# Ten slab rests of the memory stage moved from VectorE to GpSimd (one core, fp32 in two halves)

## The chip, the cores and the metric

One core of one Trainium2 chip runs the whole kernel. The metric is the device time of one execution in microseconds (us). The kernel before was timed three times; the median is what the change is held against.

## The reference, cut to what matters

The model has two blocks of two layers each. In both layers of the second block the tokens attend to a memory of 256 rows, and the part of the reference that the change touches is the making of that memory's keys and values:

```python
def rmsnorm(x, g):
    y = x * lax.rsqrt(jnp.mean(x * x, axis=-1, keepdims=True) + EPS)
    return y * g

def mem_attention(xq, mem_n, w_mem_kv):      # mem_n (1, 256, 1024), w_mem_kv (1024, 1024)
    mk, mv = jnp.split(mem_n @ w_mem_kv, 2, axis=-1)   # keys and values, 512 columns each
    ...

def even_layer(h, mem_n, ...):               # odd_layer alike
    u = rmsnorm(h, g)                        # the next stage multiplies u
    ... xq, ... = split(u @ w_in)
    m = mem_attention(xq, mem_n, w_mem_kv)
```

`mem_n @ w_mem_kv` doesn't depend on `h`, so it is computed while the norm of `h` (512 tokens by 1024 features) is made ready.

## The kernel before, in words

**Products in halves.** Each fp32 product is three TensorE products of fp32r tiles: the high half of the weights by the high half of the input, high by rest, rest by high (`product`, L477 to L482). The high half is a rounded copy made by ScalarE; the rest is the value less the high half.

**The weight stream.** All weights pass through the core as one stream of 473 slabs of 128x1024 fp32. Four engines handle each slab n in turn. SyncE loads it into `ring` (three places, L406) once the rest of slab n-3 is made. ScalarE casts it into `w_hi` (three places, `high`, L432) once TensorE has finished slab n-3. An engine subtracts, `w_lo = ring - w_hi` ("the rest of the slab"), and signals `split_done`. TensorE waits for `split_done` (`slab`) and multiplies. So the casts and rests run up to three slabs ahead of TensorE. GpSimd makes the rests (`low` and `lows_upto`, L455), but ten of them are made by VectorE with `low_by_vector` (L465), and all ten are in the stage described next, five in each layer.

**The stage around the change** is `mem_keys_values` (L2315), once in each layer of the second block. It uses eight slabs: four of the keys (24 products of 256 columns each) and four of the values (12 products of 512 columns each). Call them slabs 0 to 7 of the stage, and slabs 8, 9 and 10 the first three of the next stage. When the stage begins, the rests of slabs 0 to 2 are made or under way, so the stage itself has to issue those of slabs 3 to 10. Before the change VectorE makes the rests of slabs 3 to 7 and GpSimd those of slabs 8, 9 and 10, after a wait for VectorE's last.

Nothing schedules the engines at run time: each runs its own list, in the order in which the program wrote it.

- VectorE: the last sums of squares of `h` (`Sums.add`, L611; add 1 to add 7, written by the stage before); rest of slab 3; the reciprocal of the norm's root (`invert`, L633); rest of slab 4; then for each of eight norm tiles c a **scale** (`scale`, L785: `h` by gain by `inv` into one of two `raw` buffers) and a **norm rest** (`rest`, L791: `raw` less its rounded copy, which makes `x_ready`), with the rests of slabs 5, 6 and 7 after norm rest 1, 3 and 5.
- ScalarE: the cast of a slab once TensorE is through with the slab three before it, the copy of a finished product out of PSUM (L2368, L2383), the square root of the sum (L627), and the **round** of each norm tile (L777), which waits for its scale. Rounds 0 and 1 stand ahead of the cast of slab 6, rounds 2 and 3 ahead of slab 7's, 4 and 5 ahead of slab 8's, 6 and 7 ahead of slab 9's.
- TensorE: slabs 0 and 1, then the sum over partitions (`total`, L619, which waits for add 7), then slabs 2 to 7.
- GpSimd: the rests of slabs 8, 9 and 10.

**The next stage** (`dense_f` with `paced`, called by `mem_attention`) multiplies slabs 8 and 9 by the normalised tiles, alternating the two slabs tile by tile. It can do three products with slab 8 and then needs slab 9. Tile c also waits for norm rest c.

```python
            for i in range(2):                                    # ScalarE, values
                k.high(act, first + nk + i + 1 + SPLIT)
                norm.round(act, 4 + 2 * i)
                norm.round(act, 5 + 2 * i)
```

Of the kernel before, what the change touches and what calls it, by code (L numbers as in the profile page):

```python
# [22 lines left out]
F32 = mybir.dt.float32  # L23
# [13 lines left out]
RING = 3  # L37
SPLIT = 3
# [244 lines left out]
class Signal:  # L283


    def __init__(self, handle):
        self.handle, self.base = handle, 0
# [26 lines left out]
class Core:  # L314


    def __init__(self, nc, ctx, dram):
        self.nc, self.dram = nc, dram
        self.ctx = ctx
        sb = lambda n, s, dt=F32: ctx.enter_context(nc.sbuf_tensor(n, s, dt))  # L320
        self.ring = sb("ring", [P, RING, SLAB])
        self.w_hi = sb("w_hi", [P, SPLIT, SLAB], F32R)
        self.w_lo = sb("w_lo", [P, SPLIT, SLAB], F32R)
        self.h = sb("h", [P, KT, SEQ])
        self.x_hi = sb("x_hi", [P, KT, SEQ], F32R)
        self.x_lo = sb("x_lo", [P, KT, SEQ], F32R)
        self.r_hi = sb("r_hi", [P, 2, SEQ], F32R)
        self.r_lo = sb("r_lo", [P, 2, SEQ], F32R)
        self.inv = sb("inv", [P, SEQ])
        self.mem_hi = sb("mem_hi", [P, KT, NMEM], F32R)  # L330
        self.mem_lo = sb("mem_lo", [P, KT, NMEM], F32R)
        self.cst = sb("cst", [P, CONST_N])
        self.vec = sb("vec", [P, VEC_TOTAL])
        self.arena_n = (nc.sbuf_top - nc.sbuf_base) // 4 - 8
        self.arena = sb("arena", [P, self.arena_n])
        self.ps = ctx.enter_context(nc.psum_tensor("ps", [P, 8, SEQ], F32))
        names = ("product_done", "evacuated", "squares_done", "pairs_done", "sum_done", "root_done", "vec_chain",
                 "pool_chain", "act_step", "dve_step", "pe_step", "pe_step2", "pool_step", "dve_read", "scores_done",
                 "biased", "exp_done", "diag_done", "turned", "turned_copied", "out_done", "out_copied", "tmp_ready",
                 "high_done", "split_done", "raw_done", "hi_done", "lo_done", "x_ready", "h_written", "row_part",  # L340
                 "row_done", "row_read", "conv_gated", "conv_done", "conv_copied", "conv_squared", "conv_silu", "mix_done", "inverted", "cmp_copied", "pool_copied", "row_high", "row_low", "cst_loaded", "vec_loaded", "bias_loaded", "feed_high", "feed_ready", "feed_squared", "feed_added",
                 "feed_summed", "feed_rooted", "feed_inverted", "gate_scaled", "up_scaled", "frev_negated", "frev_made", "frev_copied",
                 "lam_dots", "lam_sum", "lam_exp", "mem_squared", "mem_summed",
                 "mem_rooted", "mem_inverted", "mem_scaled", "mem_rounded", "mem_ready", "p_high", "p_low", "proj_done",
                 "proj_part", "proj_read", "rope_swapped", "rope_added", "roped")
        self.s = {n: Signal(ctx.enter_context(nc.semaphore(n))) for n in names}
        self.slab_loaded = [ctx.enter_context(nc.semaphore(f"slab_loaded{i}")) for i in range(RING)]
        self.x_loaded = [ctx.enter_context(nc.semaphore(f"x_loaded{i}")) for i in range(4)]
        self.aux = Signal(ctx.enter_context(nc.semaphore("aux_loaded")))
        self.stored = Signal(ctx.enter_context(nc.semaphore("stored")))  # L350
        self.cmp_loaded = [Signal(ctx.enter_context(nc.semaphore(f"cmp_loaded{i}"))) for i in range(2)]
        self.loaded = self.highs = self.lows = 0
        self.lows_taken = None
        self.slab_end = []
        self.early, self.early_after, self.late = [], [], []
        self.bank_read = [None] * 8
# [91 lines left out]
    def lows_upto(self, pool, upto):  # L448

        while self.lows < min(NSLAB, upto):  # L450
            n = self.lows
            if n == self.lows_taken:
                pool.wait_ge(self.s["split_done"].handle, n)
            pool.wait_ge(self.s["high_done"].handle, n + 1)
            self.nc.gpsimd.tensor_tensor(self.w_lo[:, n % SPLIT, :], self.ring[:, n % RING, :],  # L455
                                         self.w_hi[:, n % SPLIT, :].bitcast(F32),
                                         ALU.subtract).then_inc(self.s["split_done"].handle, 1)
            self.lows += 1

    def low_by_vector(self, dve):  # L460

        n = self.lows
        dve.wait_ge(self.s["split_done"].handle, n)
        dve.wait_ge(self.s["high_done"].handle, n + 1)
        self.nc.vector.tensor_tensor(self.w_lo[:, n % SPLIT, :], self.ring[:, n % RING, :],  # L465
                                     self.w_hi[:, n % SPLIT, :].bitcast(F32),
                                     ALU.subtract).then_inc(self.s["split_done"].handle, 1)
        self.lows = self.lows_taken = n + 1

    def slab(self, pe, n, *shape):  # L470

# [1843 lines left out]
def mem_keys_values(k, layer, ready, norm, sums):  # L2315

    nc, s = k.nc, k.s  # L2320
    mk, mv = k.at(MEM_KV[layer], 4, NMEM), k.at(MEM_KV[layer] + 1024, 2, 512)
    first, nk = STREAM_AT[f"mk{layer}"]
    groups = contraction_groups(512)
    assert STREAM_AT[f"mv{layer}"] == (first + nk, len(groups))
    n = nk + len(groups)
# [5 lines left out]
    with Stage(nc) as block:  # L2331
        @block.sync
        def _(sp):
            k.stream(sp)

        @block.tensor
        def _(pe):
            pe.wait_ge(*ready)
            for m in range(nk):
                hi, lo = k.slab(pe, first + m, P)  # L2340
                k.bank(pe, m)
                for c in range(KT):
                    ins = k.product(k.ps[:, m, 0:NMEM], (hi[:, c, :], lo[:, c, :]), (k.mem_hi[:, c, :], k.mem_lo[:, c, :]),
                                    c == 0, c == KT - 1)
                ins.then_inc(done.handle, 1)
                if m == 1:
                    sums.total(pe, 6)
            for i, (c0, cn) in enumerate(groups):
                hi, lo = k.slab(pe, first + nk + i, 512)
                for t in range(2):  # L2350
                    tok = slice(t * P, (t + 1) * P)
                    if i == 0:
                        k.bank(pe, nk + t)
                    for ci in range(cn):
                        c = c0 + ci
                        ins = k.product(k.ps[:, nk + t, :], (k.mem_hi[:, c, tok], k.mem_lo[:, c, tok]),
                                        (hi[:, ci, :], lo[:, ci, :]), c == 0, c == KT - 1)
                    if i == len(groups) - 1:
                        ins.then_inc(done.handle, 1)
                if i < len(groups) - 1:  # L2360
                    ins.then_inc(part.handle, 1)

        @block.scalar
        def _(act):
            for m in range(nk):
                act.wait_ge(done.handle, done.at(m + 1))
                k.high(act, first + m + 1 + SPLIT)
                nc.scalar.copy(mk[:, m, :], k.ps[:, m, 0:NMEM]).then_inc(read.handle, 1)  # L2368
                if m == 1:
                    sums.sqrt(act, 6)  # L2370
                if m >= 2:
                    norm.round(act, 2 * m - 4)
                    norm.round(act, 2 * m - 3)
            for i in range(2):
# [3 lines that stand above are left out]
            k.high(act, first + nk + 3 + SPLIT)  # L2378
            for t in range(2):
                act.wait_ge(done.handle, done.at(nk + t + 1))  # L2380
                if t == 1:
                    k.all_high(act)
                nc.scalar.copy(mv[:, t, :], k.ps[:, nk + t, :]).then_inc(read.handle, 1)  # L2383

        @block.vector
        def _(dve):
            assert k.lows == first + SPLIT
            k.low_by_vector(dve)
            sums.invert(dve)
            k.low_by_vector(dve)  # L2390
            norm.scale(dve, 0)
            for c in range(1, KT):
                norm.scale(dve, c)
                norm.rest(dve, c - 1)
                if c % 2 == 0:
                    k.low_by_vector(dve)
            norm.rest(dve, KT - 1)

        @block.gpsimd
        def _(pool):  # L2400
            k.low(pool)
# [506 lines left out]
```

## Time and profile before

| what | value |
|---|---|
| median of 3 runs | 3308.28 us (3301.98 to 3309.21) |
| the profiled execution's own time | 3297.97 us |
| its span, first to last instruction | 3296.6 us |
| busy: TensorE, VectorE, ScalarE, GpSimd | 96%, 41%, 35%, 35% |
| mean granted TensorE clock | 0.968 of full speed |

All times in rows are us from the span's start unless marked ns. The profiled execution is 10.3 us under the median. TensorE is busy for 96% of the span. The other engines matter where TensorE waits for them, and for the change that means two stretches: from about 2175 to 2210 (first layer of the second block) and from about 2608 to 2645 (second layer).

### The profile page before, as it was taken

To read this page: it belongs to the slowest core of one execution; us is meant where nothing else is said; L and a number is where in the kernel's file an instruction comes from. 1 tells how busy PE (TensorE), PEld (TensorE's weight loads), DVE (VectorE), ACT (ScalarE), POOL (GpSimd) and SP (SyncE) were. 2 spreads that over 40 slices of the span, in tenths; PEclk is the share of its full clock that TensorE was granted. 3 is DMA by queue.
4 is the path that set the end of the run, shared out by engine and by line. 5 is a ranking of instruction groups with operands and counts; after the bars stand their busy time and mean duration, and the time that the engine had idled before them with its cause. 6 is when DMAs were issued, how large, how long until landed. Compare 5 with 4: busy or idle time off the path is not lost.

```text
span 3296.6 us, 36185 instructions
## 1 busy us (share of the span) xinstructions
PE 3149.0 (96%) x14236; PEld 2514.4 (76%) x14236; DVE 1364.8 (41%) x2455; ACT 1168.3 (35%) x2028; POOL 1147.7 (35%) x480
## 2 busy tenths in 40 slices
PE   8999998989999999999989999989999989999998
PEld 6888776668888878887758888867758768876786
DVE  5311496844121451113964321367153423156442
ACT  4222464333222442223414232344323432345422
POOL 4444431014444444444414444433314332300143
PEclk9999998799999999999999999999999999979999
DMA  4333221003333323332303333333213334300032
GB/s 141 102 96 97 81 83 39 1 26 102 96 98 98 93 89 96 98 98 89 102 21 114 97 96 101 95 97 108 86 38 97 99 104 159 96 1 1 20 96 76
DMA packets 76524, 274.33 MB, mean 83 GB/s; under 512 B 8472, under 2 KB 9368, under 8 KB 75973
## 3 DMA queue, kind: packets, MB, share of 16 engines
q1 hardware_dynamic: 76356, 272.03, 26.6%
q8 instruction: 114, 1.87, 0.2%
q14 instruction: 54, 0.43, 0.0%
HBM read 269.85 MB, written 2.15 MB: 83 GB/s over the span
## 4 chain that ended last, share of the span: by engine, by line
PE 84%; DVE 11%; ACT 2%; issue 2%; POOL 1%; DMA 0%; SPq 0%; ACTq 0%; DVEq 0%; POOLq 0%
PE ps L480 23%; PE ps L481 23%; PE ps L482 23%; PE ps L1479 5%; PE ps L1453 4%; DVE arena L2101 3%; PE ps L1467 1%; PE ps L1465 1%; DVE arena L1735 1%; PE ps L2671 1%; PE ps L2533 1%; POOL w_lo L455 0%; ACT w_hi L432 0%; PE ps L2484 0%; DVE arena L1724 0%
## 5 line engine op out<-in xcount | busy, mean ns | idle before, releaser
L455 POOL TENSOR_TENSOR w_lo<-ring,w_hi 128x1024 fp32r<-128x1024 f32 x463 | 1131.9, 2447 | 2123.9 <-ACT w_hi L432 2082.4
L480 PE MATMUL ps<-x_hi,w_hi 128*128 128x512 f32 x2168 | 860.3, 397 | 34.2 <-POOL w_lo L455 21.1
L481 PE MATMUL ps<-x_lo,w_hi 128*128 128x512 f32 x2168 | 849.4, 392 | 0.0
L482 PE MATMUL ps<-x_hi,w_lo 128*128 128x512 f32 x2168 | 849.1, 392 | 0.0
L432 ACT CAST w_hi<-ring 128x1024 fp32r<-128x1024 f32 x473 | 493.9, 1046 | 746.7 <-PE ps L482 741.8
L480 PEld LDWEIGHTS ps<-x_hi,w_hi 128*128 128x128 f32 x2168 | 410.7, 189 | 128.4 <-issue 19.6
L481 PEld LDWEIGHTS ps<-x_lo,w_hi 128*128 128x128 f32 x2168 | 410.6, 189 | 88.6 <-issue 4.4
L482 PEld LDWEIGHTS ps<-x_hi,w_lo 128*128 128x128 f32 x2168 | 410.4, 189 | 86.6
L480 PE MATMUL ps<-r_hi,w_hi 128*128 128x512 f32 x1120 | 437.4, 391 | 11.5 <-issue 11.5
L481 PE MATMUL ps<-r_lo,w_hi 128*128 128x512 f32 x1120 | 436.7, 390 | 0.0
L482 PE MATMUL ps<-r_hi,w_lo 128*128 128x512 f32 x1120 | 436.5, 390 | 0.0
L1052 DVE TENSOR_TENSOR r_lo<-arena,r_hi 128x512 fp32r<-128x512 f32 x136 | 100.9, 746 | 566.8 <-ACT r_hi L1047 566.8
L1047 ACT CAST r_hi<-arena 128x512 fp32r<-128x512 f32 x136 | 83.8, 621 | 484.8 <-PE ps L482 484.8
L480 PEld LDWEIGHTS ps<-r_hi,w_hi 128*128 128x128 f32 x1120 | 211.0, 188 | 56.3 <-issue 12.3
L482 PEld LDWEIGHTS ps<-r_hi,w_lo 128*128 128x128 f32 x1120 | 210.9, 188 | 44.2
L481 PEld LDWEIGHTS ps<-r_lo,w_hi 128*128 128x128 f32 x1120 | 211.0, 188 | 43.5
L1309 DVE TENSOR_TENSOR arena<-ps,inv 128x512 f32<-128x512 f32 x88 | 60.9, 692 | 375.4 <-PE ps L482 375.4
L1281 ACT ACTIVATE arena<-arena 128x512 f32<-128x512 f32 x88 | 55.6, 632 | 408.5 <-DVE arena L1307 408.5
L1557 ACT ACTIVATE arena<-arena 128x256 f32<-128x256 f32 (+7 forms) x240 | 120.8, 504 | 215.4 <-DVE arena L1500 214.1
L1479 PE MATMUL ps<-arena 128*128 128x128 f32 (+3 forms) x1024 | 184.6, 309 | 12.7 <-ACT arena L1566 12.7
L1453 PE MATMUL ps<-arena 128*128 128x256 f32 (+11 forms) x480 | 173.8, 453 | 5.3 <-ACT arena L2417 3.4
L1307 DVE TENSOR_TENSOR arena<-ps,inv 128x512 f32<-128x512 f32 x88 | 60.8, 691 | 285.3 <-PE ps L482 285.2
(240 smaller groups left out, 3311.5 us busy)
## 6 DMA issues: line engine op xcount, KB each, us to landing
ring<-in_stream SPq DMA_DIRECT2D x473, 512.0 KB, 3.5
arena<-in_cmp_w SPq DMA_DIRECT2D x16, 512.0 KB, 4.5
arena<-frev SPq DMA_DIRECT2D x1, 3072.0 KB, 14.8
h<-in_x SPq DMA_DIRECT2D x4, 512.0 KB, 7.1
out<-arena SPq DMA_DIRECT2D x4, 512.0 KB
arena<-in_p SPq DMA_DIRECT2D x2, 512.0 KB
arena<-in_mem SPq DMA_DIRECT2D x1, 1024.0 KB
arena<-in_pool_recip SPq DMA_DIRECT2D x1, 1024.0 KB
```

Of the source, the lines that this page charges most:

```text
L432: self.nc.scalar.copy(self.w_hi[:, n % SPLIT, :], self.ring[:, n % RING, :]).then_inc(self.s["high_done"].handle, 1)
L455: self.nc.gpsimd.tensor_tensor(self.w_lo[:, n % SPLIT, :], self.ring[:, n % RING, :], self.w_hi[:, n % SPLIT, :].bitcast(F32), ALU.subtrac ...
L480: nc.tensor.matmul(out, a[0], b[0], start=start, stop=False)
L481: nc.tensor.matmul(out, a[0], b[1], start=False, stop=False)
L482: return nc.tensor.matmul(out, a[1], b[0], start=False, stop=stop)
L1047: k.nc.scalar.copy(k.r_hi[0:w, i % 2, :], self.x[0:w, self.order[i], :]).then_inc(self.his.handle, 1)
L1052: k.nc.vector.tensor_tensor(k.r_lo[0:w, i % 2, :], self.x[0:w, self.order[i], :], k.r_hi[0:w, i % 2, :].bitcast(F32), ALU.subtract).then_i ...
L1309: nc.vector.tensor_tensor(up[:, f % 2, :], k.ps[:, 2 * (f % 3) + 1, :], inv, ALU.mult).then_inc(up_scaled.handle, 1)
L1453: nc.tensor.matmul(k.ps[:, i % 4, 0:u.w], u.q, u.key, start=True, stop=True).then_inc(scored.handle, 1)
L1479: ins = nc.tensor.matmul(k.ps[0:v.shape[-1], 6 + g % 2, 0:P], v, pt[0:rows, i % 2, j * P:(j + 1) * P], start=(u.first and j == 0), stop=(u ...
L1557: nc.scalar.activation(ex[:, i % 5, 0:u.w], ex[:, i % 5, 0:u.w], ACT.Exp, bias=low[:, i % 5:i % 5 + 1], scale=-1.0, accum_out=tot[:, i % 5 ...
L2101: k.vlink(nc.vector.scalar_tensor_tensor(dst, src, tap_weight(c, tap), dst, ALU.mult, ALU.add))
```

## The change

The three calls of `low_by_vector` in the stage (one before the reciprocal, one after it, one in the loop) go, and so do the function and its bookkeeping. GpSimd's `low`, which always continues from the last rest issued, then makes the rests of slabs 3 to 10 in one sequence, as it does in every other stage. VectorE's list in the stage is the reciprocal, eight scales and eight norm rests. The arithmetic is the same.

```diff
             n = self.lows
-            if n == self.lows_taken:
-                pool.wait_ge(self.s["split_done"].handle, n)
             pool.wait_ge(self.s["high_done"].handle, n + 1)
             self.nc.gpsimd.tensor_tensor(self.w_lo[:, n % SPLIT, :], self.ring[:, n % RING, :],
                                          self.w_hi[:, n % SPLIT, :].bitcast(F32),
                                          ALU.subtract).then_inc(self.s["split_done"].handle, 1)
             self.lows += 1
-
-    def low_by_vector(self, dve):
-
-        n = self.lows
-        dve.wait_ge(self.s["split_done"].handle, n)
-        dve.wait_ge(self.s["high_done"].handle, n + 1)
-        self.nc.vector.tensor_tensor(self.w_lo[:, n % SPLIT, :], self.ring[:, n % RING, :],
-                                     self.w_hi[:, n % SPLIT, :].bitcast(F32),
-                                     ALU.subtract).then_inc(self.s["split_done"].handle, 1)
-        self.lows = self.lows_taken = n + 1
...
         @block.vector
         def _(dve):
-            assert k.lows == first + SPLIT
-            k.low_by_vector(dve)
             sums.invert(dve)
-            k.low_by_vector(dve)
             norm.scale(dve, 0)
             for c in range(1, KT):
                 norm.scale(dve, c)
                 norm.rest(dve, c - 1)
-                if c % 2 == 0:
-                    k.low_by_vector(dve)
             norm.rest(dve, KT - 1)
```

## Rows read from the trace of the kernel before

**Rows 1.** The page, part 4: shares of the chain that ended last.

```profile
PE 84%; DVE 11%; ACT 2%; issue 2%; POOL 1%; DMA 0%; SPq 0%; ACTq 0%; DVEq 0%; POOLq 0%
```

**Rows 2.** Tile w_lo on VectorE, and line 455 on GpSimd: durations in ns, min/median/max.

```profile
L465 DVE TENSOR_TENSOR w_lo<-ring,w_hi x10: 1224/1225/1227, 2179.7 to 2633.9; 128x1024 fp32r<-128x1024 f32 x10
...
L455 POOL TENSOR_TENSOR w_lo<-ring,w_hi x463: 2339/2398/2924, 9.3 to 3265.0; 128x1024 fp32r<-128x1024 f32 x155
```

**Rows 3.** Timeline of TensorE, instructions that waited: start, duration, [idle before <- releaser].

```profile
2186.80 0.50 PE L480 MATMUL ps<-w_hi,mem_hi 128*128 128x512 f32 x1 [0.23 <-DVE w_lo L465]
2191.49 0.50 PE L480 MATMUL ps<-w_hi,mem_hi 128*128 128x512 f32 x1 [1.68 <-DVE w_lo L465]
...
2205.10 0.47 PE L480 MATMUL ps<-x_hi,w_hi 128*128 128x512 f32 x1 [1.87 <-POOL w_lo L455]
...
2640.92 0.47 PE L480 MATMUL ps<-x_hi,w_hi 128*128 128x512 f32 x1 [1.88 <-POOL w_lo L455]
```

**Rows 4.** Timeline of VectorE, first layer: one turn of its list, and the reciprocal.

```profile
2182.13 3.35 DVE L633 RECIPROCAL inv<-arena 128x512 f32<-128x512 f32 x1 [1.25 <-ACT arena L627]
...
2190.21 1.22 DVE L465 TENSOR_TENSOR w_lo<-ring,w_hi 128x1024 fp32r<-128x1024 f32 x1
2191.35 0.74 DVE L785 SCALAR_TENSOR_TENSOR arena<-h,vec,inv 128x512 f32<-128x512 f32 x1
...
2194.12 1.23 DVE L465 TENSOR_TENSOR w_lo<-ring,w_hi 128x1024 fp32r<-128x1024 f32 x1
```

**Rows 5.** Timeline of ScalarE, first layer: casts of slabs 5, 6, 9 and a table load.

```profile
2180.11 1.28 ACT L627 ACT_TABLE_LOAD   x1
...
2183.81 1.05 ACT L432 CAST w_hi<-ring 128x1024 fp32r<-128x1024 f32 x1 [1.71 <-PE ps L482]
...
2188.63 1.05 ACT L432 CAST w_hi<-ring 128x1024 fp32r<-128x1024 f32 x1
...
2200.49 1.05 ACT L432 CAST w_hi<-ring 128x1024 fp32r<-128x1024 f32 x1
```

**Rows 6.** Timelines of GpSimd and VectorE where the two meet, first layer.

```profile
2175.67 2.67 POOL L455 TENSOR_TENSOR w_lo<-ring,w_hi 128x1024 fp32r<-128x1024 f32 x1 [2.96 <-ACT w_hi L432]
2199.34 8.40 POOL L455 TENSOR_TENSOR w_lo<-ring,w_hi 128x1024 fp32r<-128x1024 f32 x3 [21.00 <-DVE w_lo L465]
...
2176.15 3.47 DVE L611 TENSOR_TENSOR arena<-arena 128x512 f32<-128x512 f32 x2
...
2199.18 0.75 DVE L785 SCALAR_TENSOR_TENSOR arena<-h,vec,inv 128x512 f32<-128x512 f32 x1
2199.84 5.66 DVE L791 TENSOR_TENSOR x_lo<-arena,x_hi 128x512 fp32r<-128x512 f32 x2
```

**Rows 7.** Timelines elsewhere: a reciprocal and a GpSimd rest at the same time.

```profile
381.11 3.35 DVE L744 RECIPROCAL inv<-arena 128x512 f32<-128x512 f32 x1 [4.72 <-ACT arena L720]
...
382.08 2.34 POOL L455 TENSOR_TENSOR w_lo<-ring,w_hi 128x1024 fp32r<-128x1024 f32 x1 [2.91 <-ACT w_hi L432]
```

**Rows 8.** Lines 785 and 667, both scalar_tensor_tensor: ns, min/median/max.

```profile
L785 DVE SCALAR_TENSOR_TENSOR arena<-h,vec,inv x32: 745/753/755, 384.5 to 2635.0; 128x512 f32<-128x512 f32 x32
...
L667 DVE SCALAR_TENSOR_TENSOR x_lo<-h,vec,x_hi x8: 740/744/2866, 7.7 to 16.9; 128x512 fp32r<-128x512 f32 x8
```

**Rows 9.** Timelines, second layer: the seven adds and the rest of slab 2.

```profile
2608.18 7.10 DVE L611 TENSOR_TENSOR arena<-arena 128x512 f32<-128x512 f32 x7
...
2612.16 2.56 POOL L455 TENSOR_TENSOR w_lo<-ring,w_hi 128x1024 fp32r<-128x1024 f32 x1 [6.44 <-ACT w_hi L432]
```

**Rows 10.** The page, part 6: the stream's loads: KB each, median us to landing.

```profile
ring<-in_stream SPq DMA_DIRECT2D x473, 512.0 KB, 3.5
```

**Rows 11.** Stretches: window, its us, TensorE busy (instructions), granted clock, DMA share, GB/s.

```profile
2202.90:2205.10 2.20, 0.33 (x3) 1.00 0.80 229
2206.30:2209.50 3.20, 3.20 (x9) 0.51 0.64 189
...
2641.00:2645.00 4.00, 4.00 (x18) 1.00 0.64 149
```

More of the change, by code:

```diff
@@ L352, in __init__ @@
         self.loaded = self.highs = self.lows = 0
-        self.lows_taken = None
         self.slab_end = []
```

## The prediction

> **What bounds the kernel now.** I began with the chain that ended last: TensorE holds 84% of it and VectorE 11% [rows 1]. So outside the change's two stretches nothing can move, and inside them only what makes TensorE wait counts. The timeline of TensorE comes next. TensorE needs 4.69 - 1.68 = 3.0 us for a slab of the values and then stands still until VectorE's rest arrives; and at the start of the next stage it waits 1.87 and 1.88 us for GpSimd's rest of slab 9, at 2205.10 and 2640.92 [rows 3]. These two starts are the yardstick of the whole forecast: everything after them hangs on them, everything before is inside them.
>
> What sets their time is a loop of two engines. VectorE's turn (slab rest, scale, norm rest, scale, norm rest) takes 2194.12 - 2190.21 = 3.91 us [rows 4], and ScalarE's next cast stands behind the two rounds that this turn feeds. Casts 6 to 9 come once in 3.91 to 4.0 us ((2200.49 - 2188.63) / 3 = 3.95) [rows 5]. A slab rest fills 1.14 us of the turn, from its start to the next scale [rows 4].
>
> **A property of the two engines that decides the case** is in the rows where they meet. A GpSimd rest takes 2.40 us alone (median) [rows 2]. At 2175.67 one started while VectorE was in an add; it took 2.67. The two adds behind it took 3.47 and end at 2179.62, 1.28 after GpSimd's end (2178.34): both ran after it, at some 0.6 to 0.7 each [rows 6]. At 2199.34 three GpSimd rests took 8.40, 2.80 each, and two norm rests took 5.66, 2.83 each [rows 6]. So the two run one at a time and take turns: VectorE's tile waits out the GpSimd rest (ends 0.55 after it), GpSimd's next rest, already waiting, waits out that tile (0.4), and goes ahead of VectorE's next. A reciprocal reads a single tile of SBUF, and ran 3.35 us beside a GpSimd rest of 2.34, neither longer than alone [rows 7].
>
> **The change, part by part.** Removed: ten VectorE rests of 1.225 us = 12.3 us [rows 2], with their waits. Added: ten GpSimd rests of 2.40 = 24 us. GpSimd has the time (it stood idle 21.00 us before 2199.34 [rows 6]); the question is whom it holds up. Removing alone would cut VectorE's turn to 3.91 - 1.14 = 2.77 us. But a turn now has a GpSimd rest in it. I replay the lists of the engines with the durations above and the rule of turns. The same replay of the kernel before gives 2205.08 and 2640.95 for the two starts, measured 2205.10 and 2640.92 [rows 3].
>
> First layer:
> - Rest 3 is issued on GpSimd at 2178.4, right behind rest 2. Add 6 is ahead of it, so it runs 2178.8 to 2181.2, and add 7 waits it out: it ends at 2181.7 instead of 2179.6. The sum on TensorE and slab 2 start 2.1 later. ScalarE's root waited for its table until 2180.11 + 1.28 = 2181.39 before [rows 5], and now comes right after the sum, 2183.0, so the reciprocal ends 1.6 later, at 2187.05 (was 2182.13 + 3.35 = 2185.48 [rows 4]).
> - Slab 2's later end puts cast 5 at 2185.9 (was 2183.81 [rows 5]). Rest 5 runs 2187.0 to 2189.4, just before scale 0 wants to start at 2187.1; scale 0 ends at 2190.0. Scale 1, rounds 0 and 1 and cast 6 follow: cast 6 ends at 2192.3 (was 2188.63 + 1.05 = 2189.68 [rows 5]). +2.6.
> - Now the turn: cast ends; GpSimd waits for the norm rest in progress (0.35); rest 2.40; the blocked scale 0.62; its round 0.62, less 0.1 of overlap; cast 1.05. Sum 4.9 to 5.0 instead of 3.95. Three turns bring cast 9's end to 2207.0 (was 2200.49 + 1.05 = 2201.54). +5.5.
> - Rest 9 starts at once, 2207.1 to 2209.5 (before it queued behind rest 8 and a norm rest, which gives 1.0 back). TensorE starts at 2209.6. **+4.5.**
>
> Second layer:
> - Here rest 2 itself (2612.16, 2.56) already holds add 7: seven adds take 7.10 [rows 9]. Rest 3 comes after add 7. No loss on the sum; rests 3 and 4 run beside sum and reciprocal, which are not held up [rows 7].
> - Rest 5 (2622.6 to 2625.0) holds norm rest 0, and rest 6, waiting, goes ahead of scale 2 (2625.4 to 2627.8). Cast 7 ends at 2631.4, 1.9 later. Two turns of 4.9 bring cast 9 to 2641.2, then rest 9 to 2643.6 and TensorE to 2643.8. **+2.9.**
>
> TensorE's products are hidden in this: a slab of the values takes 3.0 us of a 4.9 us turn. The norm tiles are ready in time: the last norm rest would end near 2206.8 and 2640.9, before the starts. SyncE's loads wait for the rest three slabs back, which moves: slab 6's goes out at 2181.2 and is needed at 2191, slab 9's goes out at 2195 and is needed at 2206; a load lands 3.5 us after its issue [rows 10], so this queue costs nothing. No DMA is added and no queue is passed; the later engines only shift.
>
> **TensorE's clock.** After 2.2 us almost without work the clock was 0.51 of full speed (the 1.2 GHz level of 2.4) from 2206.30 to 2209.50, nine products where 3.2 / 0.227 = 14 fit at the full rate of one in 0.227 us: some 1.6 us lost. In the second layer TensorE stood 1.88 us and the clock stayed at 1.00 [rows 3, 11]. After the change it would stand about 4 us before each start. The first layer has the loss already; the second gets it new. Bounds 0 (the second layer's row) and +1.6 (the first's); I take +1.5, by the first row, as 4 us is nearer to 2.2 than to 1.9. Half clock inside the stage is covered by the turn's slack of 1.9 us.
>
> **Sum:** 4.5 + 2.9 + 1.5 = +8.9 us. Against the profiled execution that is 3297.97 + 8.9 = 3306.9; that execution lies 10.3 under the median, which is outside even the lowest run, so I put the difference on the median: 3308.28 + 8.9 = 3317.2, +0.27%. About 0.2% (6.6 us) is what a measurement of this kernel can tell from no change.
>
> **What before doesn't show** is a scale (L785) held up by GpSimd: 32 of them took 745 to 755 ns [rows 8]. Bounds: not held up, and not holding GpSimd, gives +1.9 and +0.9 in the replay, 2.8 in all; held up gives 7.4. I take the latter: L667 is the same instruction, also with two tiles in SBUF, and has one of 2866 ns; and the GpSimd rest that met a scale at 2199.34 was in a group of three at 2.80 each [rows 6, 8]. The Trainium skill ("SBUF — State Buffer", section "Who interferes with whom") says that a VectorE instruction with two SBUF inputs excludes a GpSimd instruction that reads SBUF, whatever its operation; by that the scale is held up, and no row of a blocked L785 is there to agree.
>
> **Rivals.**
> - *Scales slip past* (chance 0.17): +2.8, with 0 to 1.5 of clock, 3311 to 3313. For: L785's even durations. Against: L667.
> - *No clock loss in the second layer* (0.13): 7.4, 3315.7.
> - *An unlucky meeting in the second layer* (0.12): if add 6 ends just after rest 2 is issued rather than as now, or cast 3 comes while an add waits, rest 3 gets in front of add 7 as in the first layer. The point is where the adds stand against rest 2, some 0.4 us of shift. The replay then gives +5.0 instead of +2.9: 11.0 in all, 3319.3.
> - *Faster: the turns of VectorE and GpSimd interleave without blocking* (0.08). VectorE has 2.77 us of work in a turn, GpSimd 2.40; if the tiles fall into GpSimd's gaps, or the blocking seen is rarer than the rule says, the turn falls to TensorE's own 2.9 to 3.0 and the stage is 4.7 us shorter in each layer: -9.4, 3298.9. It decides if less than about a quarter of the tiles in the loop are blocked: a turn gains 1.14 and loses some 2.2 with each blocked scale. For: GpSimd waits for a cast each time, so it has gaps. Against: the cast comes exactly when VectorE has the next scale ready, so they meet in every turn; and the meetings in [rows 6] all cost the full wait.
> - *The change doesn't do what it says* (0.02): GpSimd's rests would stay 463.
>
> **How the numbers follow.** The forecast itself has 0.48. Slower: 0.44 of it (the rest is lost to the runs' own spread), the unlucky meeting's 0.12 and half of the case at 7.4, 0.07: 0.63. Faster: 0.08. Same: 0.29, the slipping scales above all. Range: from 2.8 less half the spread of the runs, 3.6, to 11.0 plus as much: 3307 to 3323, which leaves out the faster rival and tails.
>
> **What would show each step.** GpSimd's L455 x473, L465 gone. In the first layer an add of 2.7 us or more near 2179 and the reciprocal 1.6 later. L785 with a maximum near 2.9 us and about eight blocked ones; casts 6 to 9 about 4.9 apart; the next stage's first wait 4 us long, on GpSimd, at 2209.6 and (with the first layer's shift) 2648.3; clock 0.5 after both. I am wrong if casts stay 3.9 apart or less, or if L785 stays at 755 ns.

## The result and the profile after

The changed kernel takes 3309.13 us (median of 13 runs, 3303.43 to 3312.32), the kernel before in the same series 3301.98 (13 runs, 3299.35 to 3309.21). The ratio is 1.0020, with a 95% interval of 1.0012 to 1.0029: slower, by 4 to 9.6 us. The forecast was +8.9 us and 3317.2; the medians are 7.15 us apart. In a later series it was 1.0021 (1.0012 to 1.0031). The profiled execution took 3310.14 us with a span of 3308.8, against 3297.97 and 3296.6 before.

The line numbers have moved by up to 20: 455 is 452 now, 785 is 772, 791 is 778, 633 is 620, 611 is 598, 432 is 431, 480 is 467. The first fence has the answer to [rows 2] and [rows 8], by line and in ns (min/median/max): GpSimd's rests, the scales and the norm rests.

```profile
L452 POOL TENSOR_TENSOR w_lo<-ring,w_hi x473: 2337/2397/3144, 9.8 to 3277.2; 128x1024 fp32r<-128x1024 f32 x158
...
L772 DVE SCALAR_TENSOR_TENSOR arena<-h,vec,inv x32: 746/754/2895, 385.7 to 2646.1; 128x512 f32<-128x512 f32 x32
...
L778 DVE TENSOR_TENSOR x_lo<-arena,x_hi x32: 677/683/2474, 387.1 to 2649.5; 128x512 fp32r<-128x512 f32 x32
```

GpSimd makes all 473 rests, 2.40 us each as before. No scale was above 755 ns before; now the longest is 2895. The timeline of VectorE in the first layer answers to [rows 4] and [rows 6]:

```profile
2181.43 5.50 DVE L598 TENSOR_TENSOR arena<-arena 128x512 f32<-128x512 f32 x2
2189.37 3.35 DVE L620 RECIPROCAL inv<-arena 128x512 f32<-128x512 f32 x1 [2.45 <-ACT arena L614]
2192.76 1.42 DVE L772 SCALAR_TENSOR_TENSOR arena<-h,vec,inv 128x512 f32<-128x512 f32 x2
2194.52 2.47 DVE L778 TENSOR_TENSOR x_lo<-arena,x_hi 128x512 fp32r<-128x512 f32 x1 [0.34 <-ACT x_hi L764]
2197.03 2.77 DVE L772 SCALAR_TENSOR_TENSOR arena<-h,vec,inv 128x512 f32<-128x512 f32 x1
...
2203.21 2.72 DVE L772 SCALAR_TENSOR_TENSOR arena<-h,vec,inv 128x512 f32<-128x512 f32 x1
2205.86 0.68 DVE L778 TENSOR_TENSOR x_lo<-arena,x_hi 128x512 fp32r<-128x512 f32 x1
2206.57 0.75 DVE L772 SCALAR_TENSOR_TENSOR arena<-h,vec,inv 128x512 f32<-128x512 f32 x1
2207.24 0.68 DVE L778 TENSOR_TENSOR x_lo<-arena,x_hi 128x512 fp32r<-128x512 f32 x1
2207.96 2.73 DVE L772 SCALAR_TENSOR_TENSOR arena<-h,vec,inv 128x512 f32<-128x512 f32 x1
```

The same stretch on GpSimd (its rests of slabs 2 to 10 begin at 2180.95):

```profile
2180.95 8.19 POOL L452 TENSOR_TENSOR w_lo<-ring,w_hi 128x1024 fp32r<-128x1024 f32 x3 [2.96 <-ACT w_hi L431]
2193.77 2.67 POOL L452 TENSOR_TENSOR w_lo<-ring,w_hi 128x1024 fp32r<-128x1024 f32 x1 [4.64 <-ACT w_hi L431]
2196.65 2.60 POOL L452 TENSOR_TENSOR w_lo<-ring,w_hi 128x1024 fp32r<-128x1024 f32 x1 [0.21 <-ACT w_hi L431]
2202.87 2.52 POOL L452 TENSOR_TENSOR w_lo<-ring,w_hi 128x1024 fp32r<-128x1024 f32 x1 [3.62 <-ACT w_hi L431]
2207.62 2.52 POOL L452 TENSOR_TENSOR w_lo<-ring,w_hi 128x1024 fp32r<-128x1024 f32 x1 [2.23 <-ACT w_hi L431]
```

Read the two side by side: each of the rests of slabs 5 to 8, the last four of these lines, holds up exactly one tile of VectorE. The rest at 2207.62 starts while a norm rest is in progress (until 2207.92), takes 2.52 us, 0.12 more than one alone, and ends at 2210.14; the scale of 2207.96 ends 0.55 after it, at 2210.69. Two scales and two norm rests, which took 2.77 us without a slab rest, now fill 2207.96 - 2203.21 = 4.75 us. The casts of slabs 5 to 9 on ScalarE are the answer to [rows 5]; from cast 7 on they follow that beat:

```profile
2192.64 1.05 ACT L431 CAST w_hi<-ring 128x1024 fp32r<-128x1024 f32 x1 [3.37 <-PE ps L469]
...
2195.52 1.05 ACT L431 CAST w_hi<-ring 128x1024 fp32r<-128x1024 f32 x1 [0.52 <-PE ps L469]
...
2201.75 1.04 ACT L431 CAST w_hi<-ring 128x1024 fp32r<-128x1024 f32 x1
...
2206.49 1.04 ACT L431 CAST w_hi<-ring 128x1024 fp32r<-128x1024 f32 x1
...
2211.25 1.04 ACT L431 CAST w_hi<-ring 128x1024 fp32r<-128x1024 f32 x1
```

TensorE's starts with slab 9, in both layers, answer to [rows 3]:

```profile
2214.85 0.77 PE L467 MATMUL ps<-x_hi,w_hi 128*128 128x512 f32 x1 [3.68 <-POOL w_lo L452]
...
2652.96 0.77 PE L467 MATMUL ps<-x_hi,w_hi 128*128 128x512 f32 x1 [3.68 <-POOL w_lo L452]
```

In the second layer it is scale 1 (in the group of two at 2630.93) and scale 2 that the first two rests of the loop hold up:

```profile
2631.40 2.54 POOL L452 TENSOR_TENSOR w_lo<-ring,w_hi 128x1024 fp32r<-128x1024 f32 x1 [2.29 <-ACT w_hi L431]
2636.18 2.56 POOL L452 TENSOR_TENSOR w_lo<-ring,w_hi 128x1024 fp32r<-128x1024 f32 x1 [2.23 <-ACT w_hi L431]
...
2630.93 3.56 DVE L772 SCALAR_TENSOR_TENSOR arena<-h,vec,inv 128x512 f32<-128x512 f32 x2
...
2636.52 2.77 DVE L772 SCALAR_TENSOR_TENSOR arena<-h,vec,inv 128x512 f32<-128x512 f32 x1
```

The stretches behind the starts answer to [rows 11]; between TensorE's column and the clock stand weight loads, VectorE, ScalarE and GpSimd:

```profile
2214.85:2218.00 3.15, 3.15 (x8) 2.47 (x9) 0.00 (x0) 0.00 (x0) 2.18 (x1) 0.50 0.45 166
...
2652.96:2656.00 3.04, 3.04 (x7) 2.45 (x8) 0.00 (x0) 0.00 (x0) 2.18 (x1) 0.50 0.58 175
2656.00:2659.00 3.00, 3.00 (x9) 2.30 (x8) 0.00 (x0) 0.00 (x0) 0.00 (x0) 0.56 0.63 178
```

The wait is 3.68 us instead of 1.87, and after it the clock is 0.50 in both layers, and still 0.56 from 2656 to 2659.

**Where the 12.2 us between the two spans are.** A table load of ScalarE in the stage ahead of the first stretch comes at 2143.71 where it came at 2138.45, 5.26 us later, although the lists of the engines are the same up to there. The largest step is between the table loads at 520.11 and 683.88 before, 521.68 and 691.21 after (1.57 us later at its start, 7.33 at its end; some is given back later). Here are the two stretches, of before and then of after (us, TensorE busy, granted clock, DMA share, GB/s):

```profile
520.11:683.88 163.77, 150.87 (x765) 0.82 0.00 1
```

```profile
521.68:691.21 169.53, 157.10 (x765) 0.79 0.00 1
```

The same 765 instructions take 5.8 us longer at a lower granted clock. The changed lines don't set this: the stretch takes 163.8 us in e9, 166.4 to 166.5 in e1, e4 and e6, and 169.4 to 169.6 in all the other runs, and kernels built on the one before (e9, e1, e2) stand at all three levels. Whether it changes from one execution of a program to the next or goes with the program is not shown: the changed kernel was profiled twice and had 169.5 both times. So I don't compare spans but distances that the change can alter: **from the start of GpSimd's rest of slab 2 to TensorE's start with slab 9**, and from there to the table load of the attention (the clock's part). For before these are 2205.10 - 2175.67 = 29.43 and 2640.92 - 2612.16 = 28.76; after, 2214.85 - 2180.95 = 33.90 and 2652.96 - 2621.46 = 31.50. The change costs 4.47 and 2.74 us there. From start to table load it was 24.66 and 23.04 us and is 24.61 and 25.65.

The distance isn't free of the clock either. In the second layer of the kernel before the clock fell ahead of the sum; in e1 and e9, which have the same lists there, it didn't, and their distances are 28.04 and 27.98 instead of 28.76. The same stretch after rest 2 in the kernel before and then in e1:

```profile
2615.00:2619.00 4.00, 3.62 (x12) 0.58 0.71 184
```

```profile
2621.00:2625.00 4.00, 3.49 (x24) 1.00 0.67 161
```

So a difference of less than a microsecond between two distances can be the clock's. The changed kernel's profiles have such a fall in the second layer too, so its 2.74 compares like with like.

All kernels in one table; 23.0 in the clock columns is the value without a fall of the clock.

| kernel | distance, first layer | second layer | start to table load, first | second | median, us | ratio to before |
|---|---|---|---|---|---|---|
| before | 29.43 | 28.76 | 24.66 | 23.04 | 3300.7 to 3302.1 | 1 |
| the change | 33.90 | 31.50 | 24.61 | 25.65 | 3309.13 | 1.0020 (1.0012 to 1.0029) |
| the change again | 33.95 | 31.49 | 24.59 | 25.67 | 3308.33 | 1.0021 (1.0012 to 1.0031) |
| e1: first layer only | 34.01 | 28.04 | 24.55 | 23.02 | 3306.11 | 1.0016 (1.0006 to 1.0025) |
| e2: second layer only | 29.34 | 31.28 | 24.66 | 24.44 | 3306.64 | 1.0016 (1.0007 to 1.0025) |
| e3: norm's tiles in PSUM | 26.43 | 22.54 | 23.00 | 23.04 | 3288.40 | 0.9961 (0.9948 to 0.9973) |
| e5: inverse root in PSUM | 32.00 | 29.15 | 25.49 | 25.40 | 3305.81 | 1.0012 (1.0003 to 1.0021) |
| e8: adds first | 31.46 | 31.11 | 25.76 | 24.57 | 3309.57 | 1.0023 (1.0013 to 1.0033) |
| e7: filler | 33.91 | 30.90 | 23.07 | 23.05 | 3305.92 | 1.0012 (1.0004 to 1.0021) |
| e4: only slab 4 | 28.19 | 27.84 | 23.03 | 23.02 | 3295.29 | 0.9979 (0.9970 to 0.9987) |
| e6: PSUM, adds first | 23.79 | 23.54 | 23.00 | 23.01 | 3286.26 | 0.9952 (0.9938 to 0.9966) |
| e9: before with filler | 29.31 | 27.98 | 23.06 | 23.05 | 3298.36 | 0.9992 (0.9983 to 1.0001) |

### The profile page after: what moved, and what is told of

It reads as the page before. It is cut to its first block, busy times and chain, and to the rows that moved or that the text cites. A ratio compares the mean times of both kernels' runs of the same rounds, so it can differ in the third digit from the quotient of the medians.

```text
span 3308.8 us, 36175 instructions
## 1 busy us (share of the span) xinstructions
PE 3153.6 (95%) x14236; PEld 2519.3 (76%) x14236; DVE 1366.0 (41%) x2445; ACT 1167.8 (35%) x2028; POOL 1171.3 (35%) x490
## 3 DMA queue, kind: packets, MB, share of 16 engines
q8 instruction: 114, 1.87, 0.2%
## 4 chain that ended last, share of the span: by engine, by line
PE 84%; DVE 11%; ACT 2%; issue 1%; POOL 0%; DMA 0%; SPq 0%; ACTq 0%; DVEq 0%; POOLq 0%
PE ps L467 23%; PE ps L469 23%; PE ps L468 23%; PE ps L1466 5%; PE ps L1440 4%; DVE arena L2088 3%; PE ps L1454 2%; PE ps L1452 1%; DVE arena L1722 1%; PE ps L2651 1%; DVE arena L772 1%; PE ps L2513 1%; ACT w_hi L431 1%; PE ps L2464 0%; DVE arena L1711 0%
## 5 line engine op out<-in xcount | busy, mean ns | idle before, releaser
L452 POOL TENSOR_TENSOR w_lo<-ring,w_hi 128x1024 fp32r<-128x1024 f32 x473 | 1155.5, 2445 | 2112.4 <-ACT w_hi L431 2112.4
```

## The experiments

**Each layer alone (e1, e2).** VectorE keeps its rests in one layer: `low_by_vector` takes the slab's number and does nothing for slabs that aren't in a set, which holds slabs 3 to 7 of one layer.

```diff
-            k.low_by_vector(dve)
+            k.low_by_vector(dve, first + 3)      # returns if the slab isn't in by_vector
             sums.invert(dve)
```

e1, expected:

> The change in the first layer alone. Yardstick of every run: the distance from the start of GpSimd's rest of slab 2 to TensorE's start with slab 9, 29.43 us in the first and 28.76 us in the second layer before, 33.90 and 31.50 after. My theory (GpSimd and VectorE take turns at the tiles that read SBUF twice): first layer 33.9, second 28.8, time +4 to +5 us. Rival (the loss is TensorE's clock, lost wherever TensorE idles longer): first layer's distance as after, but hardly any time, since the clock fell there before too.

e2, expected:

> The change in the second layer alone. My theory: distances 29.4 and 31.5; time +2.7 us and whatever the clock takes, 0 to 2.6. If the clock were the larger part, this run would cost more than the first layer alone; if the turns are, less.

Measured: the distance grows only in the layer that is changed, by 4.6 and 2.5 us, as the whole change has it. In e1 the unchanged second layer has 28.04 where 28.8 was expected, by the clock as said above. The times (+0.16% each, 4.1 and 4.6 us) don't tell the layers apart: their intervals are 6 us wide. The rival of e1 (only the clock costs) has against it that e1's ratio is above 1 while its clock columns are those of before.

**The norm's tiles in PSUM (e3).** Keys of slabs 2 and 3 go to the upper halves of banks 0 and 1, so banks 2, 3 and 7 are free for the two raw tiles and the inverse root.

```diff
+    norm.raw, norm.inv = k.ps[:, 2:4, :], k.ps[:, 7, :]
...
-                    ins = k.product(k.ps[:, m, 0:NMEM], ...
+                    ins = k.product(k.ps[:, m % 2, m // 2 * NMEM:(m // 2 + 1) * NMEM], ...
...
-            sums.invert(dve)
+            sums.invert(dve, k.ps[:, 7, :])
```

> The changed kernel, but the inverse root and the two raw tiles of the norm lie in PSUM, so that a scale and a norm rest read SBUF once each. Same instructions on GpSimd, each of 2.40 us. Turns theory: nothing of the norm waits for GpSimd any more (L772 and L778 back at 0.7 to 0.8 us), only the adds do: distances 25.5 and 23.5 us, time 8 to 11 us under before, 15 or more under the change. Rival (the loss is GpSimd's longer rest on the path cast, rest, product: 2.40 for 1.23): the rests stay as long and on the same path, so the distances stay at 33 to 34 and 31 to 32 and the time at +7.

This is the run that decides between the two theories. GpSimd's work is that of the changed kernel. Timelines of VectorE and GpSimd, first layer:

```profile
2196.34 0.69 DVE L778 TENSOR_TENSOR x_lo<-ps,x_hi 128x512 fp32r<-128x512 f32 x1
2197.07 0.76 DVE L772 SCALAR_TENSOR_TENSOR ps<-h,vec,ps 128x512 f32<-128x512 f32 x1
2197.74 0.68 DVE L778 TENSOR_TENSOR x_lo<-ps,x_hi 128x512 fp32r<-128x512 f32 x1
2198.46 0.76 DVE L772 SCALAR_TENSOR_TENSOR ps<-h,vec,ps 128x512 f32<-128x512 f32 x1
2199.12 0.68 DVE L778 TENSOR_TENSOR x_lo<-ps,x_hi 128x512 fp32r<-128x512 f32 x1
...
2195.63 2.42 POOL L452 TENSOR_TENSOR w_lo<-ring,w_hi 128x1024 fp32r<-128x1024 f32 x1 [0.47 <-ACT w_hi L431]
2198.36 2.42 POOL L452 TENSOR_TENSOR w_lo<-ring,w_hi 128x1024 fp32r<-128x1024 f32 x1 [0.31 <-ACT w_hi L431]
2201.08 2.41 POOL L452 TENSOR_TENSOR w_lo<-ring,w_hi 128x1024 fp32r<-128x1024 f32 x1 [0.30 <-ACT w_hi L431]
```

Tiles and rests overlap freely, at 0.7 and 2.4 us, and the rests come every 2.73 us, which is TensorE's own 12 products of 0.227. The distances shrink by 7.5 and 9.0 us against the changed kernel. The rival would have left them. They are 26.43 and 22.54 where 25.5 and 23.5 were expected: in the first layer the clock fell twice ahead of the loop, in the second not at all, which may be the reason. The kernel is 0.39% faster than the one before, 13.7 us where 8 to 11 were expected; its stretches account for 10.9 of them (3.0 and 6.2 of distance, 1.7 of clock), and the rest isn't traced. No run puts the norm's tiles in PSUM in the kernel before, so how much of the gain needs the moved rests is not shown. Against the change it comes to 3288.40 - 3309.13 = -20.7 us: 7.5 + 9.0 of distance, 1.6 + 2.6 of clock.

**Only the inverse root in PSUM (e5).** Of the diff above only what concerns `inv`.

> The changed kernel with only the inverse root in PSUM: a scale reads SBUF once, a norm rest still twice. Turns theory: L772 never over 0.8 us, L778 takes the waits now; distances 30.9 and 29.2, time +1 to +4 us over before. Rival (GpSimd's longer rest): 33.9 and 31.5, +7.

By line and form (busy us, mean ns): the scales of the stage take 748 ns as in any other stage, and the norm rests of all stages 1052 on average where 683 is a free one; they take the waits. In the timelines eight norm rests of the two layers take 2.09 to 2.21 us.

```profile
L778 DVE TENSOR_TENSOR x_lo<-arena,x_hi 128x512 fp32r<-128x512 f32 x32 | 33.7, 1052 | 1.1 <-ACT x_hi L764 0.9
...
L772 DVE SCALAR_TENSOR_TENSOR arena<-h,vec,ps 128x512 f32<-128x512 f32 x16 | 11.8, 748 | 0.5
```

The distances are 32.0 and 29.15 (expected 30.9 and 29.2), 1.9 and 2.35 less than the change's. The first is a miss by 1.1 us. Its place can be told: rest 5 starts 12.84 us after rest 2, as with the change (12.82), and from there to TensorE's start it is 19.16 us in both layers, where the change had 21.08 and 21.56. So the loop gives back less in the first layer than I expected, and rest 2 to rest 5 is as it was.

The Trainium skill says (page "SBUF — State Buffer", section "Who interferes with whom") that a VectorE instruction with at most one SBUF input, outside its two-port modes, doesn't contend with GpSimd, and one with two contends with a GpSimd instruction that reads SBUF. The runs agree for this pair of operations: 2895 ns at most for a scale with two, at most 756 ns for each of e3's 16 with one.

**Adds first (e8).**

```diff
         def _(pool):
+            pool.wait_ge(sums.added.handle, sums.added.at(KT - 1))
             k.low(pool)
```

> The changed kernel with one wait more: GpSimd starts the stage's rests only when VectorE's last add is done. Tests the first step of my working, that rest 3 gets in front of add 7 in the first layer and costs 2.1 us there. Theory: first layer's distance 33.9 - 2.1 = 31.8, second unchanged at 31.5 (there rest 3 comes after add 7 anyway), time +5 over before. Rival (add 7's delay is covered elsewhere): 33.9.

The first distance is 31.46, 2.4 less than with the change; the second 31.11. The reciprocal begins 6.39 us after rest 2 instead of 8.42, so the meeting of rest 3 and add 7 costs about the 2.1 us that were said, in the first layer alone. TensorE waits 1.20 us for the sum instead of 3.24, and its clock doesn't fall on slab 2 (1.00 from 2185.2 to 2189.2), so the clock has a part in the 2.4. The time doesn't show it: 3309.57, 7.4 over before where 5 were expected; the interval of the ratio is 6 us wide, and the clock columns sum to the same as for the change.

**Filler (e7, e9).** Spare products into an unused bank while TensorE waits: 12 in the changed kernel, 6 in the one before. They are no part of the result.

```diff
+                        if (c, m) == (0, 1):
+                            k.bank(pe, 7)
+                            for i in range(4):               # 2 in e9
+                                k.product(k.ps[:, 7, :], (hi[:, 0, :], lo[:, 0, :]), (k.x_hi[:, 0, :], k.x_lo[:, 0, :]), True, True)
                         hi, lo = k.slab(pe, first + m, P)
```

> The changed kernel, but TensorE fills the wait for slab 9's rest with 12 spare products (2.7 us) into an unused bank. The extra products are no part of the result. Tests the clock term: with the products the granted clock after the start is 1.00 in both layers instead of 0.50; distances as in the changed kernel (33.9, 31.5), the time after the starts 1.7 us (first) and 2 to 2.6 us (second) shorter, time +2 to +4 over before. Rival (the clock's fall there isn't set off by the wait, or the rows after the start aren't bound by TensorE): time as in the changed kernel, +7.

The two stretches after the starts in e7 (us, TensorE busy, granted clock, DMA share, GB/s), against 0.50 in the changed kernel:

```profile
2214.32:2218.00 3.68, 3.68 (x16) 1.00 0.62 155
2650.95:2654.00 3.05, 3.04 (x13) 1.00 0.61 177
```

From start to table load both layers have 23.1 us now, so the fall of the clock cost 1.5 and 2.6 us in the changed kernel, and the wait sets it off. The median is 3.2 us under the change's (2.4 under that of the change again), 3.8 over before, as expected. The second distance is 30.90 where 31.5 was expected: here the first rest of the loop meets norm rest 0 and not scale 1, as in e2 (31.28) and e8 (31.11).

> The kernel before, with 6 spare products (1.4 us) in TensorE's wait of 1.87 us for slab 9. They are no part of the result. Open is why the changed kernel costs 7 us on average while its stretches in one profile are 9.8 us longer. Theory A: the kernel before loses 1.6 us of clock after the second start too in most executions, and its profile showed a lucky one; then the filler takes 3 us or more off the median. Theory B: it loses only after the first, as in its profile; then 1.6 us. Distances as before in both, 29.4 and 28.8; from the start to the attention's table load 23.0 us in both layers.

e9 has 23.06 and 23.05 us, its clock 1.00 after both starts, and its ratio is 0.9992 (0.9983 to 1.0001): -2.3 us, between theory A's 3 and theory B's 1.6. It doesn't decide. The profiles speak for B as far as they go: behind a second layer with the lists of before, the start to table load is 23.04 (before) and 23.02 (e1), no fall in either. Two profiles can't say how often it falls.

**Only slab 4 (e4).** The set of VectorE's slabs is 3, 5, 6, 7 in both layers.

> The kernel before with one of five rests moved in each layer: GpSimd makes that of slab 4, while VectorE is in the reciprocal; VectorE keeps 3, 5, 6 and 7. Theory (a rest costs only where it meets a tile that reads SBUF twice, and a reciprocal doesn't): the 1.14 us of rest 4 leave VectorE's list for nothing: distances 28.3 and 27.7, time -2 us. Rival (every rest moved to GpSimd costs its 1.2 us more): distances 30.6 and 30.0.

Timelines of GpSimd and VectorE, first layer:

```profile
2183.51 2.40 POOL L458 TENSOR_TENSOR w_lo<-ring,w_hi 128x1024 fp32r<-128x1024 f32 x1 [2.62 <-DVE w_lo L469]
...
2182.20 1.23 DVE L469 TENSOR_TENSOR w_lo<-ring,w_hi 128x1024 fp32r<-128x1024 f32 x1
2184.56 3.35 DVE L636 RECIPROCAL inv<-arena 128x512 f32<-128x512 f32 x1 [1.13 <-ACT arena L630]
2187.95 1.42 DVE L788 SCALAR_TENSOR_TENSOR arena<-h,vec,inv 128x512 f32<-128x512 f32 x2
```

The rest lies beside the reciprocal, both at their own length, and scale 0 starts right behind it. Distances 28.19 and 27.84: -1.24 and -0.92. The clock didn't fall after either start, which gives another 1.6 in the first layer. The ratio is 0.9979 (0.9970 to 0.9987), faster than the kernel before, by 6.9 us in the medians where 2 were expected. The stretches account for 3.8 of them, 1.6 of which is the clock's: TensorE waited 1.88 us before both starts, as in the kernel before, where the clock fell after the first. That part may be chance, and the remaining 3 us aren't traced.

**PSUM and adds first (e6).** e3 with the wait of e8.

> Norm's tiles in PSUM as in e3, and GpSimd's first rest after the last add as in e8: no meeting left. Theory: e3's first distance less 1.6 to 2.1, 24.3 to 24.8; second as in e3 (22.5); time 1.6 to 2 us under e3, 14 to 16 under before. Rival (TensorE itself is the bound by now): distances as in e3.

First distance 23.79, 2.6 less than in e3; second 23.54, 1.0 more. The second is the clock: it was 0.57 from 2611 to 2615 here, and 1.00 at the same place of e3 (2614 to 2618). In the first layer e3 had one fall more, at 0.57 from 2186 to 2190, so there too not all of the 2.6 is the add's. 3286.26 us, 0.9952 of before (0.9938 to 0.9966): the fastest of all, 15.9 us under before and 22.9 under the change by the medians.

**The change again.**

> The changed kernel once more, beside the same runs of before: for the size of the difference, and a second profile of it. Distances 33.9 and 31.5 again if they are set by the lists of the engines; from the start to the table load 24.6 to 25.7 us, as the clock falls. Time +6 to +9 over before.

33.95 and 31.49 us, within 0.05 of the first profile, and again +0.21%.

## Why the prediction was right or wrong

- **Two-engine loop, and what bounds.** Right. The turn of scales and norm rests sets the casts, the casts set the starts.
- **Taking turns.** Right, and it is the cause of the loss: e3 keeps all of GpSimd's work and removes the meetings of the norm's tiles, and the loss turns into a gain. The bound that I had to choose, whether a scale is held up at all, fell on the side chosen: seven scales of 2.7 to 2.9 us in the two layers, and one norm rest.
- **First layer, +4.5.** Measured 4.47. But the agreement is luck: two errors inside it cancel. Counted from rest 2, the reciprocal began at 8.42 where I had 8.03, and TensorE, which had waited 3.24 us for the sum, had a granted clock of 0.70 from 2186 to 2190, slab 2's products among them, so cast 5 began 1.5 us later than in the working. "Half clock inside the stage is covered by the turn's slack" was wrong there, as the turns hadn't begun. Rest 5 thereby missed scale 0 and met norm rest 0 instead; cast 6 ended 1.0 earlier than said (2196.57 - 2180.95 = 15.62, for 2192.3 - 2175.67 = 16.6), and the next cast took 6.23 us instead of 4.9. The last two turns are 4.74 and 4.76 (4.9 said), and cast 9 ends at 31.34 after rest 2, where I had 31.3.
- **Second layer, +2.9.** Measured 2.74; the adds take 7.10 us as before, as said. The meetings are not quite the ones said: rest 5 holds scale 1 (2895 ns), not norm rest 0, and rest 6 goes ahead of scale 2 as said, but 14.7 us after rest 2 and not 13.2. Cast 7 ends 19.4 after rest 2 all the same (19.2 said), and two turns of 4.75 for 4.9 bring the total to what was said. The number is again in part luck; other profiles of this layer with the same lists up to the start have 31.28 (e2) and 30.90 (e7).
- **The clock, +1.5.** The mechanism is right (e7), the size in the second layer was 2.61 in the profile: the clock was still low after 2656, so more than the one stretch of the first layer's row was lost. In the working the 1.6 doesn't follow from nine products instead of 14 (5 x 0.227 = 1.1) but from half the clock over 3.2 us; measured for the first layer is 24.66 - 23.0 = 1.66. The medians don't bear it out in full: 4.47 + 2.74 + 2.6 = 9.8 us in the stretches, 7.15 between the medians. Behind the second table load the changed kernel's profile is 2.45 us shorter than before's (630.19 for 632.64), all of it in the two attention stages where the granted clock is a little higher:

```profile
2663.96:2773.17 109.21, 99.82 (x521) 0.94 0.38 128
...
2875.67:3112.22 236.55, 221.51 (x1182) 0.88 0.02 5
```

```profile
2678.61:2786.82 108.21, 98.58 (x521) 0.95 0.39 129
...
2889.32:3124.37 235.05, 219.80 (x1182) 0.89 0.02 5
```

  The change again has 630.1 there, but e8, whose second table load comes 11.7 us later than before, has 632.5. Whether that comes with the shift or by chance stays open; e9 was to say how often the kernel before loses its clock in the second layer, and did not.
- **The level.** This is the step that failed. "I put the difference on the median": 3308.28 was the median of three runs, with 10.3 us to the profiled execution. Thirteen runs have 3301.98, which is 6.3 lower; of the three runs, 3309.21 is the highest of the thirteen and 3308.28 the second highest. The median of three was a high draw, and the warning stood beside it: the profiled execution pointed to 3306.9, to which the measured 3309.13 is nearer. The difference forecast, +8.9 us, lies in the measured interval of 4 to 9.6, if at its upper end; put on 3301.98 it gives 3310.9 for 3309.13. Put on 3308.28 it gave 3317.2, 8 us too much, inside the range (3307 to 3323) near its lower end.
- **Slower, same or faster.** Slower is established (the interval excludes 1), over 0.2% is not: the ratio is 1.0020. The faster rival fell: its condition was that less than a quarter of the tiles in the loop are held up, and it is one tile in each turn of four, with the full wait. That condition was also stated too loosely: at 1.14 gained for each turn and 2.2 lost for each held scale, the break-even is half a hold for each turn, an eighth of the tiles. e3 shows what the rival would have been: a beat of 2.73 us, below the 2.9 to 3.0 that I took for TensorE's own.

## What to carry to other kernels

Where instructions of VectorE and GpSimd like these both read two SBUF tiles, moving work from one to the other doesn't make it parallel: count one wait of the longer instruction for each meeting, and look at the instruction that gets in front, not at busy shares. The cure that worked is to let one operand of VectorE's tiles live in PSUM, or to place GpSimd's instruction beside one that reads SBUF once, like the reciprocal. And a difference of a few us belongs on a median of many runs, or on distances between events of one stage, not on three runs.

## What the runs showed of the hardware that was not expected

- With one operand in PSUM the tiles of VectorE run at full speed beside GpSimd (0.76 and 0.68 us beside 2.42), and writing raw tiles to PSUM costs a scale nothing (756 ns for 754, medians).
- The same 765 instructions of TensorE take 163.8, 166.4 or 169.5 us in different profiles, with a granted clock of 0.82, 0.81 and 0.79. What decides between the three isn't shown.
- TensorE's clock fell to 0.50 within the wait of 3.68 us and stayed so behind the start for about 3 us (first layer) and over 5 us (second layer); with 12 spare products in the wait it didn't fall. Waits of 1.87 and 1.88 us in the kernel before had a fall in the first layer and none in the second; in e4 waits of 1.88 us had none in either.
